# One gate column a group moved to GpSimd, eight expert tiles in three fp32r passes, one DMA row issued two tiles earlier

## What is computed

```python
q = (xt @ wq).reshape(T, 8, 2, 128)                       # 8 heads, two halves
s = einsum('thpd,hpnd->thpn', q, subkeys)                 # 128 keys a half
top_s, top_i = top_k(s, 16)
best_s, best_j = top_k(all 16 x 16 sums of the two halves, 16)
idx   = take_along_axis(128 * i0 + i1, best_j)            # one of 16384 experts
gates = softmax(best_s)
hdn = gelu(einsum('cd,chkd->chk', x, u_tab[idx])) * gates
out = einsum('chk,chkd->cd', hdn, v_tab[idx])
```

## Time and profile before

| | us |
|---|---|
| median of 3 runs | 1633.8 (1632.44 to 1635.3) |
| profiled execution, own time | 1631.77 |
| its span | 1630.0 |
| PE busy | 1591.8 (98%) |
| DVE busy | 1262.1 (77%) |
| ACT busy | 871.0 (53%) |
| POOL busy | 196.7 (12%) |
| gate groups, first to last matmul pass | 463.0 to 551.1 |

### The profile page before, as it was taken

The page is one execution under the profiler, slowest core; times in us unless marked ns, Lnnn a source line. Parts: engine busy times, 40 slices in busy tenths (PEclk is TensorE's granted clock), DMA queues, the critical chain, the costliest instruction groups (busy, mean ns, idle before and its releaser), DMA issues.

```text
span 1630.0 us, 32300 instructions
## 1 busy us (share of the span) xinstructions
PE 1591.8 (98%) x11268; PEld 1412.8 (87%) x11268; DVE 1262.1 (77%) x2678; ACT 871.0 (53%) x1600; POOL 196.7 (12%) x156
## 2 busy tenths in 40 slices
PE   6999999999999999999999999999999999999998
PEld 4887989899988887788888888888899877999998
DVE  6885647959989887788888888888878365688887
ACT  3544231464569844455555555555654246566665
POOL 0020220027600000000000000000048014300000
PEclk9999999999999999999999999999999999999999
DMA  9842137847642388677777777777555651255553
GB/s 354 298 138 89 42 131 277 307 156 213 197 138 63 117 269 259 213 241 239 232 241 235 242 239 235 238 237 241 190 158 171 211 197 40 79 177 183 181 182 128
DMA packets 102623, 316.85 MB, mean 194 GB/s; under 512 B 11392, under 2 KB 21376, under 8 KB 102144
## 3 DMA queue, kind: packets, MB, share of 16 engines
q1 hardware_dynamic: 101664, 311.23, 58.1%
q10 hardware_dynamic: 864, 4.32, 0.7%
HBM read 309.61 MB, written 5.90 MB: 194 GB/s over the span
## 4 chain that ended last, share of the span: by engine, by line
PE 79%; DVE 7%; ACT 6%; issue 3%; DMA 2%; POOL 2%; SPq 0%; DVEq 0%; POOLq 0%; ACTq 0%
PE bank L520 10%; PE bank L507 9%; PE bank L508 9%; PE bank L509 9%; PE bank L2140 7%; PE bank L2142 7%; PE bank L2144 7%; PE bank L528 5%; ACT arena L2103 2%; PE bank L781 2%; PE bank L1768 2%; POOL wlo L501 2%; ACT arena L2094 2%; DVE wlo L501 1%; PE bank L1940 1%
## 5 line engine op out<-in xcount | busy, mean ns | idle before, releaser
L496 ACT CAST whi<-wring 128x1024 fp32r<-128x1024 f32 x395 | 412.9, 1046 | 176.4 <-PE bank L509 109.1
L501 DVE TENSOR_TENSOR wlo<-wring,whi 128x1024 fp32r<-128x1024 f32 x341 | 416.8, 1223 | 52.3 <-ACT whi L496 51.7
L507 PE MATMUL bank<-xboth,whi 128*128 128x256 f32 x752 | 219.0, 291 | 4.4 <-DVE wlo L501 2.2
L508 PE MATMUL bank<-xboth,whi 128*128 128x256 f32 x752 | 212.6, 283 | 0.0
L509 PE MATMUL bank<-xboth,wlo 128*128 128x256 f32 x752 | 212.6, 283 | 0.0
L520 PE MATMUL bank<-xboth,whi 128*128 128x512 f32 x704 | 188.7, 390 | 0.0
L2140 PE MATMUL bank<-whi,Whi 128*128 128x512 f32 x512 | 159.4, 392 | 4.4 <-DVE Wlo L2265 4.4
L2142 PE MATMUL bank<-wlo,Whi 128*128 128x512 f32 x512 | 158.6, 391 | 0.0
L501 POOL TENSOR_TENSOR wlo<-wring,whi 128x1024 fp32r<-128x1024 f32 x54 | 137.2, 2547 | 177.3 <-ACT whi L496 177.2
L2144 PE MATMUL bank<-whi,Wlo 128*128 128x512 f32 x512 | 157.7, 389 | 0.0
L520 PEld LDWEIGHTS bank<-xboth,whi 128*128 128x128 f32 x704 | 132.5, 188 | 24.0
(11 more groups left out here) (400 smaller groups left out, 3034.9 us busy)
## 6 DMA issues: line engine op xcount, KB each, us to landing
wring<-in_w SPq DMA_DIRECT2D x463, 512.0 KB, 3.6
arena<-in_ada SPq DMA_DIRECT2D x48, 512.0 KB, 7.2
xn<-in_ada SPq DMA_DIRECT2D x96, 256.0 KB, 3.7
h_spill<-arena SPq DMA_DIRECT2D x37, 128.0 KB, 2.0
arena<-h_spill SPq DMA_DIRECT2D x37, 128.0 KB, 4.1
wring<-in_w SPq DMA_DIRECT2D x6, 384.0 KB, 5.5
wring<-in_w SPq DMA_DIRECT2D x8, 256.0 KB, 2.6
arena<-in_const ACTq DMA_DIRECT2D x1, 1151.0 KB, 5.1
```

The lines of the kernel that those rows point to most:

```text
L496: act.copy(whi[:, n % HSLOTS, :], wring[:, n % SLOTS, :]).then_inc(hi_ready, 1)
L501: eng.tensor_tensor(wlo[:, n % SLOTS, :], wring[:, n % SLOTS, :], whi[:, n % HSLOTS, :].bitcast(F32), ALU.subtract).then_inc(lo_ready, 1)
L507: pe.matmul(out, h, xh, start=start, stop=False, **kw)
L508: pe.matmul(out, h, xl, start=False, stop=False, **kw)
```

## The change

Four edits:

1. Column three (t = 2) of each group goes from DVE to GpSimd, by the same instruction; in every fourth group (n % 4 == 3) DVE keeps three columns and GpSimd takes ACT's, so ACT has no column in that group.
2. A4 and B4 move from two of the three `whi` slots to the buffer `xn`.
3. The eight up tiles 32 to 39 run split. ACT casts tiles 32 to 34 before the gates and 35 to 39 between its work behind groups 6, 14, 22, 30 and 38 and the copy of the next group; DVE subtracts tile 32 before the gates and 34 to 39 behind groups 6, 14, 22, 30, 38 and 46; GpSimd subtracts tile 33 before its first column.
4. The `ada2` row of the first turn is issued after v tile 36 is freed, ahead of the loads that wait for v tiles 37 and 38; it stood behind both.

```diff
-        rG, _ = region(arena, S * NK + 2 * KT * S + D, [("A4", 1024), ("B4", 1024)])
+        rG, _ = region(xn_flat, 0, [("A4", 1024), ("B4", 1024)])
...
                 if j + 4 in LONE_HALVES:
                     half(LONE_HALVES.index(j + 4), 0)
+                elif j == LONE_HALVES[-1]:
+                    half(len(LONE_HALVES), 0)
             first, end, lone = u_tile(EARLY), PEER_ROUNDS - 1, len(LONE_HALVES)
-            half(lone, 0)
...
             for j in range(EXP_AFTER, TURN_AFTER):
                 act_early(act, j)
+                if 0 <= j - 28 < HSLOTS:
+                    n = P0 + j - 28 + TURN_AFTER
+                    act_hi(act, n, count_at(n), None)
...
+            n = P0 + TURN_AFTER
+            dve.wait_ge(lo_ready, nth_split[n] - 1)
+            tile_lo(dve, n, nth_split[n])
             dve.wait_ge(t3_turned, 1)
...
-                for t in range(3):
+                for t in range(3 if n % 4 == 3 else 2):
                     ins = dve.tensor_scalar(B4[:, b, t, :], rG["iota"], ...)
                 ins.then_inc(hot, 1)
+                if n in LO_AT:
+                    if LO_AT[n] == 2:
+                        dve.wait_ge(lo_ready, nth_split[P0 + TURN_AFTER + 1])
+                    tile = P0 + TURN_AFTER + LO_AT[n]
+                    tile_lo(dve, tile, nth_split[tile])
+
+        HI_AT = {8 * i - 18: i for i in range(HSLOTS, EARLY - TURN_AFTER)}
+        LO_AT = {8 * i - 10: i for i in range(2, EARLY - TURN_AFTER)}
+        def pool_hot(pool):
+            n = P0 + TURN_AFTER + 1
+            pool.wait_ge(lo_ready, nth_split[n] - 1)
+            tile_lo(pool, n, nth_split[n])
+            pool.wait_ge(t3_ready, 1)
+            for n in range(GROUPS):
+                b, t0 = n % 2, 4 * n
+                if n >= 2:
+                    pool.wait_ge(g_ready, n - 1)
+                t = 3 if n % 4 == 3 else 2
+                pool.tensor_scalar(B4[:, b, t, :], rG["iota"], ...).then_inc(hot_pool, 1)
...
+        def pe_late_early(pe, j, k):
+            n = P0 + j
+            if k == 0:
+                pe.wait_ge(lo_ready, nth_split[n])
+                pe.wait_ge(h_early, j - 2)
+            mm = three(pe, bank[j % 3][:, 0:S], n, k, xhi[:, k, :], xlo[:, k, :], k == 0, k == KT - 1)
+            if k == KT - 1:
+                mm.then_inc(tile_done, 1)
...
                 pe.wait_ge(hot, n + 1)
-                pe.wait_ge(hot_act, n + 1)
+                pe.wait_ge(hot_pool, n + 1)
+                if n % 4 != 3:
+                    pe.wait_ge(hot_act, n - n // 4 + 1)
...
-                if n + 2 < GROUPS:
+                if (n + 2) % 4 != 3 and n + 2 < GROUPS:
                     act_hot(act, n + 2)
+                if n in HI_AT:
+                    j = TURN_AFTER + HI_AT[n]
+                    act_hi(act, P0 + j, count_at(P0 + j), P0 + j - HSLOTS + 1)
```

More of the change, by code:

```diff
@@ L79 @@
 EARLY_PLAIN = 14
+EARLY_TURN = 32
 GATE_SPLIT = 7
@@ L487, in build_layer_pair @@
         split_tiles = [FIRST[name] + k for name in SPLIT for k in range(SPLIT2 if name == "w_in2" else COUNT[name])
-                       if k >= SKIP.get(name, 0) or (name == "peer" and k < EARLY_SPLIT and k != EARLY_PLAIN)]
+                       if k >= SKIP.get(name, 0) or (name == "peer" and k != EARLY_PLAIN and not EARLY_SPLIT <= k < EARLY_TURN)]
         nth_split = {n: i + 1 for i, n in enumerate(split_tiles)}
@@ L1924, in act_route @@
                 act_early(act, j)
+                if 0 <= j - 28 < HSLOTS:
+                    n = P0 + j - 28 + TURN_AFTER
+                    act_hi(act, n, count_at(n), None)
         ranks, rank_wide = sem("ranks"), sem("rank_wide")
-        EXP_AFTER, TURN_AFTER = 25, 32
+        EXP_AFTER, TURN_AFTER = 25, EARLY_TURN
         h_early = sem("h_early")
@@ L2066, in dve_hot @@
                 ins.then_inc(hot, 1)
+                if n in LO_AT:
[5 more added lines that the diff above has]
+        LO_AT = {8 * i - 10: i for i in range(2, EARLY - TURN_AFTER)}
+        hot_pool = sem("hot_pool")
+        def pool_hot(pool):
[8 more added lines that the diff above has]
+                t = 3 if n % 4 == 3 else 2
+                pool.tensor_scalar(B4[:, b, t, :], rG["iota"], T3[:, 1, t0 + t:t0 + t + 1],
+                                   T3[:, 2, t0 + t:t0 + t + 1], ALU.is_equal, ALU.mult).then_inc(hot_pool, 1)
         def pieces_beside(n):
@@ L2075, in pe_gates @@
                 for j, k in pieces_beside(n):
-                    pe_early(pe, TURN_AFTER + j, k, k + 1)
+                    pe_late_early(pe, TURN_AFTER + j, k)
                 pe.wait_ge(hot, n + 1)
-                pe.wait_ge(hot_act, n + 1)
+                pe.wait_ge(hot_pool, n + 1)
+                if n % 4 != 3:
+                    pe.wait_ge(hot_act, n - n // 4 + 1)
                 if n >= 4:
@@ L2088, in act_hot @@
         def act_hot(act, n):
-            t, away = 4 * n + 3, rG["away"][:, (n % 2) * 128:(n % 2) * 128 + 128]
-            if n >= 2:
-                act.wait_ge(hot_act, n - 1)
+            i = n - n // 4
+            t, away = 4 * n + 3, rG["away"][:, (i % 2) * 128:(i % 2) * 128 + 128]
+            if i >= 2:
+                act.wait_ge(hot_act, i - 1)
             act.activation(away, rG["iota"], ACT.Square, scale=-1.0, bias=T3[:, 1, t:t + 1]).then_inc(away_ready, 1)
-            act.wait_ge(away_ready, n + 1)
+            act.wait_ge(away_ready, i + 1)
             act.activation(B4[:, n % 2, 3, :], away, ACT.Relu, scale=rG["ngate"][:, n:n + 1],
@@ L2110, in act_gates @@
                 if n == GROUPS - 3:
-                    act_hi(act, v_tile(0), count_at(v_tile(0)), None)
+                    act_hi(act, v_tile(0), count_at(v_tile(0)), v_tile(0) - HSLOTS + 1)
         P0 = FIRST["peer"]
@@ L2222, in act_peer @@
             weigh(0)
-            act_hi(act, v_tile(1), count_at(v_tile(1)), None)
+            act_hi(act, v_tile(1), count_at(v_tile(1)), v_tile(1) - HSLOTS + 1)
             weigh(1)
@@ L3283, in _ @@
             pool_route(pool)
+            pool_hot(pool)
             pool_pairs(pool)
```

## The result

The changed kernel took 1636.66 us (median of 20 runs, 1634.47 to 1638.56), the kernel before beside it 1633.05 us (20 runs, 1630.32 to 1636.84). The ratio is 1.0022, with a 95% interval of 1.0016 to 1.0029: about 3.6 us slower. The profiled execution has a span of 1633.1 us against 1630.0, both at a granted clock of 0.999.

The account below looks back on a forecast made before the run. The prediction took round trips over two buffers, by ACT or DVE, to bound the gates. Gates +3.8, GpSimd +0.3 and row -3.1 gave +1.0 on 1633.8: 1634.8 us, own range 1632 to 1637, 8 in 10 within 1628.5 to 1643.5.

Parts of the forecast that it names:

- the ground: Gates: time of eight groups without inserted casts and subtractions, put at 10.8 us instead of 11.08.
- What bounds the kernel: Gates: three engines in one period, plus round trips over two buffers, 2.64 us by ACT and 2.74 by DVE.
- Columns: Gates: DVE loses a column in 48 of 64 groups, yet eight groups fall only 0.3 us, to 10.8.
- the cover: Gates: the time DVE's lost columns could win, said to go at once because ACT is late next.
- Subtraction and cast: Gates: inserted work delays PE by 0.75 and 0.35 us a round, making 11.9 instead of 11.08.
- GpSimd's column: Gates: sharing between GpSimd and DVE costs +0.3 us, low bound 0, high bound 13.
- rival B: Gates: DVE shuts GpSimd out until it has a gap, +5, in all +6: 1639.8 us; chance 0.30.
- Three passes for PE: Gates: a piece takes 0.36 us instead of 0.43, which gives nothing by itself as PE waits in each group.
- The row: First turn: the row issued sooner lands before DVE needs it, a kept gain of 3.1 us.
- Rival C: First turn: the row still lands late, gain 1 us or less, +3 in all: 1637 us; chance 0.08.
- Rival A: Gates: the stage follows the busiest engine, not the round trip, in all -8: 1625.7 us; chance 0.20.
- Buffers in `xn`: Gates: moving A4 and B4 to `xn` costs 0, as its readers there are done with tile 31.

Follow-up runs that it names:

- e3_columns: Kernel before with the row issued sooner and one column a group on GpSimd, plain tiles, buffers in `whi`: gates 90.3 us, ratio 0.9995.
- e5_passes: Changed kernel without edit one: DVE makes three columns and ACT one in every group, casts and subtractions stay: gates 94.3 us, ratio 1.0020.
- e2_col_twice: Changed kernel with GpSimd's column made in groups 0 and 1 only, left uncomputed afterwards: gates 94.7 us, ratio 1.0028.
- e8_one_more_wait: e1_row with one more, already satisfied semaphore wait of PE in each gate group: gates 90.5 us, ratio 0.9998.
- e1_row: Kernel before with only the first turn's row issued sooner: gates 88.1 us, ratio 0.9986.
- e9_one_wait_less: e3_columns with PE's wait for ACT's copy kept only in groups where ACT makes no column: gates 88.3 us, ratio 0.9975.
- e12_after_less: Changed kernel with PE's wait for ACT's copy kept only in groups where ACT makes no column: gates 93.6 us, ratio 1.0011.
- e4_three: Changed kernel with three buffers for A4 and B4 instead of two: gates 82.1 us, ratio 0.9945.
- e7_three_cols: e3_columns with three buffers for A4 and B4 instead of two: gates 82.9 us, ratio 0.9948.

## Why the prediction came out as it did

The forecast was +1.0 us and the change measured +3.6; the time lies inside the range. The gates were forecast 3.0 us too short, and the rest of the program was 0.4 us better than forecast. That the gates were not missed by more is partly luck: two errors in them, of the ground and of the inserts, have opposite signs.

- *What bounds the kernel.* Right, and confirmed from the other side: round trips over two buffers bound the gates as soon as DVE is relieved, and a third buffer takes them away.
- *Columns: 10.8 for eight groups.* This is the step that failed. "Then about 0.10 to PE: 2.64" carried over the lag of the kernel before. It was right for that kernel, where PE began 0.10 after a Relu that ended last. But the change itself puts in a fourth wait, and with it the lag is 0.25 and the trip 2.81. The sentence that "the cover is gone at once, because what is late next is ACT" was right; that adding a wait has a price of its own was not thought of. Eight groups without inserts take 11.40 in e3_columns and 11.53 in the changed kernel's seventh round, and 11.12 and 11.21 with one wait less. So the fourth wait is 0.3 of the missing 0.6 to 0.7 a round; of what is left, 0.05 a trip is the lag of 0.15 instead of 0.10, and the Gelu costs more; GpSimd's column is then as late as ScalarE's.
- *Subtraction and cast.* Predicted +0.75 and +0.35 a round, 11.9 with the ground. Counted from the sixth group of a round to the sixth of the next, eight groups of the changed kernel take 12.26 to 12.30 with both, 11.95 with the subtraction alone and 11.34 to 11.53 with neither. So the two cost some 0.8 a round on their own ground, not 1.1. The inserts were put 0.3 too high and the ground 0.6 to 0.7 too low. Where DVE is never idle they cost 1.03 a round (e5_passes), near the forecast; that they cost less here because ACT and DVE have idle moments is likely, but was not tested.
- *GpSimd's column: +0.3, bounds 0 and 13.* Measured 0.5, from e2_col_twice. The column takes 1.1 to 2.1 us where it took 0.374 alone, as rival B's mechanism would have it (that it waits for gaps of DVE was not tested by itself), but PE's waits name it only twice, 1.6 us, and DVE's columns hardly take longer beside it (355 ns against 340), so the two did not hold each other up alike. Rival B's size, +5, is not there: taking the column out gives 0.5.
- *Three passes for PE.* Nothing by itself, as predicted, as long as PE waits: a round without inserts takes 11.08 in e5_passes, as before. With three buffers it is worth 0.07 us a group.
- *The row: -3.1.* The rest of the program, which holds it, measured -3.05 on average over eleven kernels, and -2.3 (-3.6 to -0.8) where the row stands alone. The size was right, as far as this can tell. Rival C did not come: no PE wait of over 1 us in the first turn of the changed kernel.
- *Rival A.* Wrong for this kernel, by the direct test: in e3_columns DVE and ACT have less to do than before and nothing is inserted, and the stage got longer by 2.2 us. It becomes true with three buffers, 82.1 us with the same work.
- *Buffers in `xn`.* Not tested by itself. A round without inserts takes 11.40 in e3_columns, with the buffers in `whi` and plain pieces, and 11.53 in the changed kernel; this 0.13 was not taken apart.

Apart for a sum: of the +7.1 in the gates, 1.6 is the fourth wait and 0.5 GpSimd's sharing, by single edits to the changed kernel. The other 5.0 is left for the inserted casts and subtractions; the step from e3_columns (90.3) to the changed kernel (95.2) says 4.9. The parts do not simply add: the same inserts cost 6.2 where DVE keeps its three columns (e5_passes). With three buffers they cost 0.6 a round (10.63 against 10.0), and PE's shorter pieces give that back.

## What to carry to other kernels

Where several engines fill double buffers for one, find which trip over the buffers ends last and size each of its pieces, the lag between the last writer and the reader too; here relieving VectorE moved nothing until that trip was shorter. Count the semaphores in front of a matmul that sits on such a trip: one that is implied by another engine's own order can be left out, and a new producer brings one. If a region that is written last can lend a third buffer until then, try it together with moving work between engines: here the third buffer gave 0.8 us, the moved columns lost 2.2, and both together gave 5.2.

## What the runs showed of the hardware

- A semaphore wait that was always satisfied when the one behind it was cost 2.4 us over 64 groups (e8_one_more_wait against e1_row). The trace shows it as a second instruction of PE that only waits, 0.11 us after the first. TensorE began a group 0.25 us after ScalarE's last write with four waits (e8_one_more_wait, e3_columns, the changed kernel), 0.15 with three of which one was GpSimd's (e9_one_wait_less, e12_after_less), and 0.10 with three before; behind VectorE it was 0.23 us at the median with four and 0.11 with three.
- The profile can name a wait "issue" where ScalarE or GpSimd came last (all 25 in the changed kernel's gates stand so). It names waits so with three semaphores as well as with four, and in e8_one_more_wait it named VectorE throughout.
- GpSimd's 128x128 fp32 scaling, 0.374 us alone, took 1.3 to 1.4 us beside VectorE's chain in every kernel that has one in each group, and cost VectorE little (355 ns against 340 a column).
- With a piece of an up tile in three fp32r passes a group of the gates took 1.25 us on TensorE (e4_three), with a plain fp32 piece 1.32 (e7_three_cols).
